# Attention loop of a streaming encoder step: PE order over tiles, copies of q and k, the convolution's units and the pointwise products

## What is computed

```python
z = rms_norm(x, g_mix) @ w_in                 # q 8x64 | k 2x64 | v 2x64 | value 512 | gate 512
q, k = rms_norm(q, g_q), rms_norm(k, g_k)     # per head
u = a * sigmoid(b)
s = q @ k^T / 8 - slope * |distance|          # own chunk of 64 and 2 before it
o = softmax([s, sink]) @ v
c = causal_depthwise(u, width 31)
c = silu(layer_norm(c)) @ w_pw + b_pw         # "convolution units", then "pointwise products"
mixed = concat(rms_norm(o), rms_norm(c)) @ w_out
x = x + mixed
x = x + mixture_of_experts(rms_norm(x))       # top 1 of 4 groups, top 2 of 8 experts
x = x + sigmoid(rms_norm(x) @ w_g) * (p @ w_p)
```

## Time and profile before

| | us |
|---|---|
| median of 3 runs (1384.09 to 1388.32) | 1386.67 |
| the profiled execution, its own time | 1388.99 |
| its span on the profiler's clock | 1386.8 |
| PE busy | 1275.7 (92%) |
| DVE busy | 958.1 (69%) |
| ACT busy | 719.0 (52%) |
| POOL busy | 396.6 (29%) |

### The profile page before, as it was taken

One profiled execution on the slowest core, in us unless ns is written; L12 is line 12 of the kernel. 1 busy time (PEld: TensorE's weight loads), 2 busy tenths in 40 slices (PEclk: granted clock), 3 DMA queues, 4 the chain that ended last, 5 costly groups with the idle time before them and its releaser, 6 DMA issues.

```text
span 1386.8 us, 18160 instructions
## 1 busy us (share of the span) xinstructions
PE 1275.7 (92%) x6337; PEld 1063.3 (77%) x6337; DVE 958.1 (69%) x940; ACT 719.0 (52%) x872; POOL 396.6 (29%) x399
## 2 busy tenths in 40 slices
PE   5999878989987799987999999999999999994997
PEld 4888867767775688854788888888888888873886
DVE  4223945664565522256799999999999999996652
ACT  5224024544444222133577877877777787773221
POOL 1000014353311100002344444444444444441000
PEclk9999988988956999989999999999999999997999
DMA  7521002000001341114899999999999999995431
GB/s 273 125 59 35 1 16 91 16 16 11 4 33 61 129 152 64 66 54 162 325 393 387 365 380 383 368 378 381 379 384 396 394 397 401 392 371 205 143 100 62
DMA packets 72223, 289.54 MB, mean 209 GB/s; under 512 B 24048, under 2 KB 26800, under 8 KB 46830
## 3 DMA queue, kind: packets, MB, share of 16 engines
q1 hardware_dynamic: 61950, 271.03, 52.1%
q0 software_dynamic: 10224, 17.85, 3.4%
HBM read 276.13 MB, written 32.17 MB: 222 GB/s over the span
## 4 chain that ended last, share of the span: by engine, by line
PE 77%; DVE 7%; DMA 2%; issue 2%; ACT 1%; POOL 1%; POOLq 0%; SPq 0%; DVEq 0%; ACTq 0%
PE ps L419 20%; PE ps L421 20%; PE ps L420 20%; PE ps L1735 3%; PE ps L1854 3%; PE ps L1742 2%; PE ps L1816 1%; PE ps L1881 1%; PE ps L1866 1%; PE ps L1915 1%; PE ps L2002 1%; DVE mem L1330 1%; DVE mem L1339 1%; DVE mem L1342 1%; DVE whl L408 1%
## 5 line engine op out<-in xcount | busy, mean ns | idle before, releaser
L408 DVE TENSOR_TENSOR whl<-mem,whl 128x2048 fp32r<-128x2048 f32 (+2 forms) x219 | 491.5, 2249 | 32.8 <-ACT whl L1119 22.6
L419 PE MATMUL ps<-whl,ahl 128*128 128x512 f32 x1120 | 446.9, 399 | 7.0 <-DVE mem L1449 3.5
L1119 ACT ACTIVATE whl<-mem 128x2048 fp32r<-128x2048 f32 x202 | 387.2, 1919 | 95.7 <-PE ps L421 95.7
L420 PE MATMUL ps<-whl,ahl 128*128 128x512 f32 x1120 | 434.9, 388 | 0.0
L421 PE MATMUL ps<-whl,ahl 128*128 128x512 f32 x1120 | 434.6, 388 | 0.0
L419 PEld LDWEIGHTS ps<-whl,ahl 128*128 128x128 f32 x1120 | 216.2, 193 | 47.8 <-issue 5.4
L421 PEld LDWEIGHTS ps<-whl,ahl 128*128 128x128 f32 x1120 | 214.2, 191 | 44.0
L420 PEld LDWEIGHTS ps<-whl,ahl 128*128 128x128 f32 x1120 | 215.6, 192 | 39.5
L824 POOL DMA_INDIRECT y_rows<-mem x35 | 92.7, 2650 | 291.5 <-DVE mem L1635 290.7
L721 POOL TENSOR_SCALAR mem<-mem 128x1 f32<-128x1 f32 (+2 forms) x68 | 16.2, 238 | 489.2 <-ACT mem L898 384.4
L408 DVE TENSOR_TENSOR ahl<-ps,ahl 128x512 fp32r<-128x512 f32 (+1 forms) x106 | 88.5, 856 | 85.4 <-ACT ahl L912 36.9
(11 more groups left out here) (231 smaller groups left out, 1454.1 us busy)
## 6 DMA issues: line engine op xcount, KB each, us to landing
mem<-in_w_e_up SPq DMA_DIRECT2D x66, 1024.0 KB, 7.4
mem<-in_w_e_gate SPq DMA_DIRECT2D x66, 1024.0 KB, 7.4
mem<-in_w_e_down SPq DMA_DIRECT2D x66, 1024.0 KB, 7.9
mem<-in_x_prompt SPq DMA_DIRECT2D x24, 512.0 KB, 3.5
mem<-y_rows SPq DMA_DIRECT2D x16, 512.0 KB, 5.5
mem<-in_w_in SPq DMA_DIRECT2D x4, 1024.0 KB, 11.8
mem<-in_w_out SPq DMA_DIRECT2D x4, 1024.0 KB, 5.3
h_rows<-mem SPq DMA_DIRECT2D x8, 512.0 KB, 2.6
```

What stands on the lines that cost most here:

```text
L408: return which.tensor_tensor(out, full, hi.bitcast(F32), ALU.subtract)
L419: nc.tensor.matmul(out, act_hi, whl[:, 0, w_at], start=first, stop=False)
L420: nc.tensor.matmul(out, act_hi, whl[:, 1, w_at], start=False, stop=False)
L1119: nc.scalar.activation(whl[:, 0, slot * CH:(slot + 1) * CH], raw[c], ACT.Copy).then_inc(s_mhi, jobs)
```

## The change

- **PE order over tiles.** `qkv` is cut into four pairs of k steps. Tile t + 1's first pair now stands ahead of tile t's ten transposes; the second pair follows them, the third and fourth stand in the middle of the tile. The scores of (t, 0) stand ahead of the probability transposes of (t - 1, 1), and the input transposes run one tile further ahead (`x_turned`).
- **Raw q and k copied out.** ACT writes the squares to a buffer of their own (`sq`) and then copies q and k to SBUF (`qkn`); DVE's first multiply reads that copy. Banks 2 and 3 are free after ACT's three reads.
- **DVE order.** `biased` is split into `scores_in` and `score_stats`; `qk_norm(t + 1)` stands between the two for (t, 1).
- **Units inside the loop.** In tiles 4 to 7 two units each are turned, and their tanh, scaling and multiply done, all through bank 0; the convolution's sums, squares and norms are drawn together in tiles 0 to 3; eight buffers `c_t` hold the units.
- **Pointwise products amid the last tile.** After tile 7, `pointwise(0)` to `pointwise(8)` alternate with the attention of tile 8, with the DVE, ACT and POOL work of both interleaved; `swish_hi` and `swish_lo` of units 0 to 3 stand in tile 7.
- **Loads.** The chunks of `w_out` get buffers of their own and other due times, the late gains other places, the first expert's chunks are loaded after the chunks of `w_out` are used. One input norm (`x_norm(NT + 2)`) moves into the convolution stage.

The diff, cut to its core (of the new loops and the new tail only the added lines are shown; `pointwise_out`, `pointwise_norm`, `pointwise_square` hold the same operations as the loops that they replace):

```diff
-        c_t = [mem[:, U0 + i * C:U0 + (i + 1) * C] for i in range(4)]
-        c_junk = mem[:, U0 + 8 * C:U0 + 8 * C + C // 2]
-        c_y = [mem[:, U0 + (4 + i) * C:U0 + (5 + i) * C] for i in range(4)]
+        c_t = [mem[:, U0 + i * C:U0 + (i + 1) * C] for i in range(8)]
+        sq = raw1[1][:, 0:QW + KVW]
+        c_y = raw1[1][:, QW + KVW:QW + KVW + C]
+        o_junk = raw1[1][:, QW + KVW + C:QW + KVW + C + C // 2]
+        bpw = u2
...
+        c_t.append(xb[1][:, 0:C])
+        c_y8 = xb[1][:, C:2 * C]
+        c_junk, o_junk_late, h_junk = gmix[:, 0:C // 2], gmix[:, C // 2:C], gmix[:, C:2 * C]
+        goc = gqk[:, 0:C]
+        gffn = bias_all[:, 0:D]
+        hb = [bias_all[:, D:2 * D], kTb.rearrange("p b g k -> p (b g k)")]
+        VB0 = B0 + 2 * D + D + QW + KVW + NH * 2 * P + 2 * NKV * 2 * P
+        hT = mem[:, VB0:VB0 + D]
...
-            return raw1[i].rearrange("p (a n) -> p a n", n=D), s_raw[i], 1 if j < 2 else 6 + (j - 9) // 2
+            at = raw[j - J_OUT] if j >= J_OUT else raw1[i]
+            return at.rearrange("p (a n) -> p a n", n=D), s_raw[i], 1 if j < 2 else 6 + (j - 9) // 2
...
-                if j in (9, 10):
+                if j == 9:
+                if j == 10:
+                    sp.wait_ge(s_c2, 8)
+                    sp.wait_ge(s_ssq, NT)
-                    sp.wait_ge(s_wlv, j - 1)
+                    sp.wait_ge(signal, 16 * 6)
+                    sp.wait_ge(s_cl, 4 if j == 11 else 8)
...
-                    load_chunk(10)
+                    sp.wait_ge(s_ut, 1)
+                    sp.wait_ge(s_uos, 16)
+                    sp.dma_start(bpw, a["b_pw"][0].partition_broadcast(P)).then_inc(s_gm, 16)
...
+            sp.wait_ge(s_gm, 16 * 2)
+            sp.dma_start(goc, a["g_oc"][0].partition_broadcast(P)).then_inc(s_gm, 16)
             load_x(2 * NT)
+            load_chunk(11)
+            load_chunk(10)
+            load_chunk(12)
+            sp.wait_ge(s_sb, 2 * NT)
+            sp.wait_ge(s_gm, 16 * 3)
+            sp.dma_start(gffn, a["g_ffn"][0].partition_broadcast(P)).then_inc(s_gm, 16)
+            sp.wait_ge(s_cl, 9)
             load_x(2 * NT + 1)
-            sp.wait_ge(s_o, NT)
-            sp.wait_ge(s_kv, 16 * 6)
-            for dst, name in ((bpw, "b_pw"), (goc, "g_oc"), (gffn, "g_ffn")):
-                sp.dma_start(dst, a[name][0].partition_broadcast(P)).then_inc(s_gm, 16)
-            for j in range(11, SPLIT_JOBS):
-                load_chunk(j)
...
+            for t in range(TS):
+                if t in (2, 3):
+                    conv_rstd(2 * t - 4)
+                    conv_rstd(2 * t - 3)
+                if t in (1, 2):
+                    conv_neg_mean(2 * t - 2)
+                    conv_neg_mean(2 * t - 1)
+                if NT + t + 3 < 2 * NT:
+                    x_rstd(NT + t + 3)
                 if t >= 1:
-                    pool.wait_ge(s_osq, t)
-                    pool.wait_ge(s_o, t - 1)
-                    rstd(r1, ss1, 1.0 / C, s_ors, t)
+                    attention_rstd(t - 1)
+                pool.wait_ge(s_ssq, t + 2)
+                rstd(r10, ss10, 1.0 / HD, s_r10, t + 2)
                 sample_taps(4 * t, 4 * t + 4)
...
+            x_square(NT + 2)
             for j in range(4, J_OUT):
                 mixer_hi(act, j)
+            x_hi(NT + 1, 0, 0)
...
+                if t == 0:
+                    act.wait_ge(s_uo, 16 * PH)
+                if t >= 1:
+                    act.wait_ge(s_ssq, t)
+                nc.scalar.activation(sq, banks2(2)[:, 0:QW + KVW], ACT.Square).then_inc(s_sq, 1)
                 if t >= 1:
                     act.wait_ge(s_qkt, t)
                 if t == TS:
                     act.wait_ge(s_kv, 16 * 4)
-                nc.scalar.activation(qkn[:, 0:QW + KVW], banks2(2)[:, 0:QW + KVW], ACT.Square).then_inc(s_sq, 1)
+                nc.scalar.activation(qkn[:, 0:QW + KVW], banks2(2)[:, 0:QW + KVW], ACT.Copy).then_inc(s_zev, 1)
...
+            square_qk(0)
+            for t in range(TS):
+                qk_in_place(t)
+                if t >= 1:
+                    exps(t - 1, 1)
+                x_hi(NT + t + 1, 1, 0)
+                if t >= 1:
+                    pt_copy(t - 1, 1)
+                if t + 2 < NT:
+                    x_hi(NT + t + 2, 0, 0)
+                if NT + t + 3 < 2 * NT:
+                    x_square(NT + t + 3)
+                if t in (1, 2):
+                    for i in range(4):
+                        conv_square(4 * t - 4 + i)
+                exps(t, 0)
+                if t >= 4:
+                    conv_tanh(2 * t - 8)
+                if t >= 1:
+                    attention_square(t - 1)
+                square_qk(t + 1)
+                pt_copy(t, 0)
+                if t == TS - 1:
+                    for u in range(4):
+                        swish_hi(u)
+                if t >= 4:
+                    conv_tanh(2 * t - 7)
+
+            qk_in_place(TS)
+            exps(TS - 1, 1)
+            act.wait_ge(s_ut, 2)
+            nc.scalar.activation(R[0:SAMPLE, TS, C:2 * C], bank(0)[0:SAMPLE, :], ACT.Copy).then_inc(s_uT, 1)
+            pt_copy(TS - 1, 1)
+            pointwise_square(0)
+            conv_square(TS)
+            mixer_hi(act, J_OUT)
+            exps(TS, 0)
+            pointwise_square(1)
+            attention_square(TS - 1)
...
+                if g == 14:
+                    x_norm(NT + 2)
...
-                dve.wait_ge(s_v, t + 1)
-                dve.wait_ge(s_ssq, t + 1)
-                nc.vector.tensor_tensor(qkn[:, 0:QW + KVW].rearrange("p (h d) -> p h d", d=HD),
-                                        banks2(2)[:, 0:QW + KVW].rearrange("p (h d) -> p h d", d=HD),
-                                        r10.unsqueeze(2).broadcast_to([P, NH + NKV, HD]), ALU.mult).then_inc(s_zev, 1)
+                chain(nc.vector.tensor_tensor(qkn[:, 0:QW + KVW].rearrange("p (h d) -> p h d", d=HD),
+                                              qkn[:, 0:QW + KVW].rearrange("p (h d) -> p h d", d=HD),
+                                              r10.unsqueeze(2).broadcast_to([P, NH + NKV, HD]), ALU.mult))
...
+            x_lo(NT + 1, 0, 0)
             qk_sums(0)
             qk_norm(0)
+            for t in range(TS):
+                x_lo(NT + t + 1, 1, 0)
+                scores_in(t, 0)
+                score_stats(t, 0)
+                if t + 2 < NT:
+                    x_lo(NT + t + 2, 0, 0)
                 if t >= 1:
                     attention_out(t - 1)
+                if NT + t + 3 < 2 * NT:
+                    x_norm(NT + t + 3)
+                if t >= 4:
+                    swish(2 * t - 8)
+                qk_sums(t + 1)
+                scores_in(t, 1)
+                qk_norm(t + 1)
+                if t == TS - 1:
+                    for u in range(4):
+                        swish_lo(u)
+                score_stats(t, 1)
+                if t >= 4:
+                    swish(2 * t - 7)
                 if t >= 1:
                     attention_norm(t - 1)
+                if t in (0, 1):
+                    conv_sum(2 * t)
+                    conv_sum(2 * t + 1)
+                if t in (2, 3):
+                    conv_norm(2 * t - 4)
+                    conv_norm(2 * t - 3)
...
+            pointwise_out(0)
+            conv_sum(4)
+            pointwise_out(1)
+            scores_in(TS, 0)
+            score_stats(TS, 0)
+            pointwise_norm(0)
+            pointwise_out(2)
+            attention_out(TS - 1)
             conv_norm(4)
+            pointwise_norm(1)
+            pointwise_out(3)
+            for u in range(4, 8):
+                swish_lo(u)
+            scores_in(TS, 1)
+            score_stats(TS, 1)
+            dve_chunk(J_OUT)
...
+            x_transpose(NT + 1, 0, 0, xb[(NT + 1) % 2])
+            for pair in range(4):
+                qkv(0, pair)
+            for t in range(TS):
+                qkv(t + 1, 0)
+                qk_turned(t)
+                qkv(t + 1, 1)
+                x_turned(t, 1)
+                score(t, 0)
+                if t >= 1:
+                    prob_transpose(t - 1, 1)
+                if t + 2 < NT:
+                    x_turned(t, 0)
+                if t >= 1:
+                    attend(t - 1, 1)
+                qkv(t + 1, 2)
+                if t >= 4:
+                    turn_conv(2 * t - 8)
+                qkv(t + 1, 3)
+                prob_transpose(t, 0)
+                score(t, 1)
+                attend(t, 0)
+                if t >= 4:
+                    turn_conv(2 * t - 7)
+
+            qk_turned(TS)
+            pointwise(0)
+            pointwise(1)
+            pe.wait_ge(s_convs, 1)
+            pe.wait_ge(s_xl, 4 * NT)
+            pe.wait_ge(s_cth, 8)
+            pe.wait_ge(s_cy, 8)
+            for c in range(KC):
+                last = nc.tensor.transpose(ps[0:SAMPLE, 0, c * P:(c + 1) * P], acc[:, c, :], ident)
+            last.then_inc(s_ut, 1)
+            score(TS, 0)
```

(24 more changed lines are left out.)

407 lines of the change are left out of this document (158 added, 249 removed).

## The result

The kernel after the change takes a median of 1334.67 us (four runs, 1332.62 to 1335.3) where the kernel before, on the same chip, took 1387.49 (four runs, 1384.09 to 1389.62). The ratio is 0.9619, interval 0.9596 to 0.9642: faster by 52.8 us. The profiled execution after has a span of 1333.5 us (its own time 1335.3) against 1386.8 before. The forecast was 1330.

What follows compares the result with a forecast made beforehand. The prediction saw PE held by its wait for the second multiply of q and k and by half clock. From 1386.8 us, −31.4 (loop), +5 (clock), −32 (after tile 7) and +1.8 (entry) gave 1330, range 1314 to 1358.

Steps and rivals of the forecast that it cites:

- Step 1: Loop over eight tiles: PE's waits fall to 9.4 us in all from 27.6.
- the multiply's wait: Ten transposes waiting for DVE's second multiply of q and k: 0.3 us left in tiles 2 and 3.
- The copy's wait: Mid-tile, product with v waits for ACT's copy of the probabilities: a new wait of 0.6 us per tile.
- Step 2: Unit transposes moved into tiles 4 to 7: +3.8 us on PE; loop 166.5 at full clock, −31.4.
- Step 3: Loop: two or three falls of PE's clock, +5 us, between bounds of 0 and 17.
- Step 4: After tile 7, up to the output projection's first product: 54 us against 85.9, −32.
- the low parts: After tile 7: tile 7's low parts on DVE delay the first pointwise product by 1.4 us.
- the last bias: End of the part after tile 7: PE waits about 4 us for a bias behind two splits on DVE.
- Step 5: Entry to tile 0: input norm in DVE's convolution work and four transposes ahead, +1.8 us.
- Half clock stays: Rival: clock falls in every loop tile (17 us) and costs 17 after tile 7; 1354 us, chance 0.27.
- The order of DVE and ACT becomes the bound: Rival: bank 0 or late exponentials cost 2.5 us in seven tiles, 8 after tile 7; 1356, chance 0.11.
- The clock does not come back: Rival: half clock throughout tiles 4 to 7 and after tile 7; +59 us, 1446, chance 0.05.

Runs made afterwards that it cites:

- e4: Kernel after the change, with ACT's four convolution squares of tiles 1 and 2 moved behind the copy of the probabilities; 1327.96 us, ratio 0.9559.
- e1: Kernel after the change, with DVE's two multiplies of q and k behind the row maxima of the scores again; 1340.71 us, ratio 0.9652.
- e3: Kernel after the change, with the first pair of the next tile's product behind the ten transposes; 1350.84 us, ratio 0.9733.
- e2: Kernel after the change, without the copy of raw q and k: DVE's first multiply reads PSUM; 1337.73 us, ratio 0.9637.
- e8: Against e4, POOL's last sample taps in tile 7 moved ahead of the roots of tile 8; 1324.29 us, ratio 0.9532.
- e7: Against e4, DVE's last bias and ACT's copy of turned rows moved ahead of splitting the third output weight chunk; 1323.95 us, ratio 0.9532.
- e6: Against e4, all nine pointwise products moved behind tile 8's attention on PE, DVE, ACT and POOL; 1344.69 us, ratio 0.9685.

## Why the prediction was right

**Step 1.** Right. PE at full clock was to take 20.1 in a steady tile and has 20.14 in e4; the multiply's wait was to be 0.3 us in tiles 2 and 3 and nothing behind. It was nothing from tile 2 to tile 7, with 0.2 to 0.3 us to spare at the end of tile 3. e1 and e3 show both of its causes at work. The two multiplies, taken at 1.39 each, were 1.23 and 1.25, which is about half of that difference, and e2 and e8 show that the contention is real. The copy's wait, forecast at 0.6 a tile, is 0.68. The waits of the loop together are 175.13 − 164.90 = 10.2 for a forecast of 9.4: less in tile 0 (1.90 for 3.0), and 1.17 ahead of tile 8's ten transposes, which the prediction left out. That tile is the last: no pair of a next product stands ahead of them.

**Step 2, a term that was mis-sized.** The sixteen unit transposes of a tile were taken to halve with the clock, to 0.95. They don't. The first eight of tile 4 in the kernel after, at full clock, with the weight product behind them:

```profile
287.02 0.71 PE L1974 MATMUL ps<-mem 64*128 64x64 f32 x8
287.66 0.50 PE L422 MATMUL ps<-whl,ahl 128*128 128x512 f32 x1
```

By row starts they take 0.64, so sixteen take 1.28 where sixteen took 1.90 at half clock, and the product behind them is 0.50 where 0.40 is usual. A tile with units is 22.43 − 20.83 = 1.60 longer, so four cost 6.4 and not 3.8. PE's other work was put 1.6 too high: e4 has 158.08 busy at full clock, units at 6.4 and the rest at 151.7 for 153.3. So 157.1 of work were forecast and 158.08 measured; that the two misses nearly cancel is luck. With the 10.2 of waits of the change itself the loop at full clock would be 168.3, where 166.5 was forecast. e4's 165.85 lies nearer only because its edit removed waits that the forecast had counted (7.8 left for 9.4).

**Step 3, clock in the loop.** "Two or three falls, +5." There were two, and PE's busy time is 164.90 where the same instructions at full clock take 158.08 in e4: 6.8, inside the bounds of 0 and 17. One fall is that of tile 1. The other came in tile 7, which no edit of e4 touches. Two windows of the kernel after:

```profile
351.00:352.00 1.00, 1.00 (x12) 1.00 (x10) 0.93 (x3) 0.00 (x0) 0.00 (x0) 1.00 0.00 0
352.00:353.00 1.00, 1.00 (x5) 0.83 (x4) 0.90 (x5) 0.64 (x4) 0.00 (x0) 0.55 0.00 0
```

It followed a wait of 1.11 for the probability copy and lasted until about 355.5; e4 has tile 7 at 1.00 throughout, 1.6 shorter. That there were just two falls is in part chance: e4 and e7 have the same list in the loop, and e7's clock falls in tile 7 where e4's does not. The loop came to 175.1 where 171.5 was forecast: 0.8 by the waits, 1.0 by the work at full clock, 1.8 by the clock. That is the whole miss of the span (1333.5 for 1330.2). The median missed by 4.7, since it lay 1.2 above the span of the profiled execution where the forecast took it 0.1 below. A slip of 2 us stands in the range: 1330 less 10 is 1320, not 1318; both hold the result.

**Step 4.** 54 forecast, 54.3 measured. The agreement is closer than its terms. The waits: the low parts 1.4 forecast, 2.35 measured, since four of them take 4.39 beside POOL; the copies of probabilities 0.8 and 1.4 forecast, 0.46 and 1.61 measured; the last bias 4 forecast, 3.15 measured; and the 1.6 in small ones did not come. That is 7.6 for 9.2. PE's work and half clock together were put at 39.8 + 5 = 44.8 and came to 46.7. The clock is 0.87 where 0.9 or more was asked for: one sign of the prediction that failed. It fell early (0.65 in the first 14.6 us) and once more for 3.4 us from 407 on, behind the 1.61 wait. e6 shows the mechanism, e7 and e8 the two waits.

**Step 5.** +1.8 forecast, +1.6 measured.

**The rivals.** *Half clock stays* fell. It said that the stretch of transposes and scores would lower the clock in each tile. That stretch lasts 6.5 us and stayed at 1.00 in tiles 3 to 6 (e4: in all); the two falls in the loop came behind a wait, not behind the transposes alone. By the Trainium skill (TensorE: Matmul & The Clock Gate, Part 4: PE-mode transpose) those transposes would not have counted as busy in the same way. The trace does not bear out the consequence that the rival drew from it; with e6's 0.58, where attention stands without weight products for 30 us and PE idles 8.3 of them, the rule and idling cannot be told apart. *The order of DVE and ACT becomes the bound* fell as a whole, and was right in two places, both of them terms of the forecast too: the late exponentials of tiles 1 and 2 (1.65 and 0.77 us), which e4 took away, and the late last bias (3.15), of which e7 left 0.8. *The clock does not come back* fell: tiles 4 to 6 have 1.00, and tile 7 is back at it after 3.4 us.

## What to carry to other kernels

When PE waits at the end of a chain that runs over three engines, move work on both sides: independent PE work ahead of the wait, and on the engine that closes the chain the closing step ahead of work that nobody waits for. Here the one gave 13 to 16 us and the other 6 to 10. Then read, one by one, each wait of one or two us that is left: tile 1, with a wait of 1.65 us and half clock behind it, took 6.5 us more than without both, and four such reorderings of two to six lines took another 22 us. A list order on an engine far from the critical path (POOL's taps) can be one of them. And compare the clock by place before a small difference is put down to an edit: it fell at different places in executions whose lists on PE were the same.
